# The scan's triangular inverse: block transposes on VectorE instead of TensorE, and b scaled to the chunk's end by GpSimd

## What is computed

```python
def step(state, inp):
    r_t, w_t, k_t, v_t, a_t, b_t = inp
    sa = jnp.einsum('bhij,bhj->bhi', state, a_t)
    state = (state * w_t[:, :, None, :] + sa[..., None] * b_t[:, :, None, :]
             + v_t[..., None] * k_t[:, :, None, :])
    return state, jnp.einsum('bhij,bhj->bhi', state, r_t)
```

## Time and profile before

| what | value |
|---|---|
| median of 3 runs | 1724.61 us (1722.05 to 1726.17) |
| span of the profiled execution | 1724.5 us, which is its own time from first to last instruction |
| TensorE busy | 1670.0 us, 97% |
| VectorE busy | 1327.7 us, 77% |
| ScalarE, GpSimd busy | 696.7 us, 614.6 us |
| mean granted TensorE clock | 0.991 |

### The profile page before, as it was taken

How to read it: one execution, slowest core, us unless ns; L and a number is a source line. 1 busy time by engine, 2 the same in 40 slices (tenths; PEclk the granted TensorE clock), 3 DMA queues, 4 the chain that set the end, 5 groups by cost and what they waited for, 6 DMA issues and landing times.

```text
span 1724.5 us, 29253 instructions
## 1 busy us (share of the span) xinstructions
PE 1670.0 (97%) x11467; PEld 1472.8 (85%) x11467; DVE 1327.7 (77%) x2704; ACT 696.7 (40%) x1056; POOL 614.6 (36%) x393
## 2 busy tenths in 40 slices
PE   9999899988999999999999999999999999999997
PEld 7877469977888898999989999999999998777886
DVE  5654665576599998999926667888888888887777
ACT  4112752233333344888833333333333333333334
POOL 0000011000376664332342235656556555442120
PEclk9999999999999999999999999999999999999999
DMA  6220010021323353566497788999999999999994
GB/s 241 97 93 17 1 51 4 4 111 57 115 101 115 121 161 130 194 231 247 175 369 277 237 306 332 354 372 350 339 353 371 354 340 323 356 387 334 328 314 175
DMA packets 128040, 380.89 MB, mean 221 GB/s; under 512 B 12064, under 2 KB 52384, under 8 KB 126880
## 3 DMA queue, kind: packets, MB, share of 16 engines
q1 hardware_dynamic: 81104, 207.28, 33.8%
q0 software_dynamic: 37728, 159.40, 25.0%
q10 hardware_dynamic: 9072, 12.35, 2.0%
HBM read 339.92 MB, written 39.06 MB: 220 GB/s over the span
## 4 chain that ended last, share of the span: by engine, by line
PE 45%; DVE 11%; DMA 4%; ACT 0%; issue 0%; POOL 0%; SPq 0%; DVEq 0%; ACTq 0%; POOLq 0%
PE ps L203 15%; PE ps L205 15%; PE ps L204 15%; DVE gated_cols L2130 5%; DMA mixed<-hidden_ahead 3%; DVE wout_raw L2130 3%; DVE wout_raw L2133 2%; PE ps L2248 1%; DMA gates<-gate_matrix 1%; DVE v_lo L2183 0%; DVE h L2205 0%; ACT v_hi L2094 0%; DVE h L2212 0%; POOL u_lo L1990 0%; DVE h L2153 0%
## 5 line engine op out<-in xcount | busy, mean ns | idle before, releaser
L203 PE MATMUL ps<-v_hi,a_hi 128*128 128x512 f32 x768 | 301.5, 393 | 10.7 <-DVE a_lo L2186 7.9
L204 PE MATMUL ps<-v_lo,a_hi 128*128 128x512 f32 x768 | 300.8, 392 | 0.0
L205 PE MATMUL ps<-v_hi,a_lo 128*128 128x512 f32 x768 | 300.6, 391 | 0.0
L2007 POOL DMA_INDIRECT v_selected<-in_v,expert_index x128 | 186.3, 1456 | 298.2 <-DVE h L2153 284.0
L203 PE MATMUL ps<-xn_hi,u_hi 128*128 128x384 f32 (+1 forms) x800 | 275.0, 344 | 9.3 <-DVE xn_lo L1425 3.7
L204 PE MATMUL ps<-xn_lo,u_hi 128*128 128x384 f32 (+1 forms) x800 | 272.1, 340 | 0.0
L205 PE MATMUL ps<-xn_hi,u_lo 128*128 128x384 f32 (+1 forms) x800 | 272.0, 340 | 0.0
L2183 DVE TENSOR_TENSOR v_lo<-wout_raw,v_hi 128x1024 fp32r<-128x1024 f32 x128 | 156.6, 1223 | 99.5 <-ACT v_hi L2094 98.4
L1998 POOL DMA_INDIRECT u_selected<-in_u_rows,expert_index x128 | 181.7, 1419 | 142.0 <-DVE hidden_selected L2140 114.7
L2094 ACT ACTIVATE v_hi<-wout_raw 128x1024 fp32r<-128x1024 f32 x128 | 135.0, 1054 | 137.4 <-PE ps L205 137.4
L203 PEld LDWEIGHTS ps<-v_hi,a_hi 128*128 128x128 f32 x768 | 145.1, 189 | 41.4 <-DVE v_lo L2183 12.8
(11 more groups left out here) (329 smaller groups left out, 3102.7 us busy)
## 6 DMA issues: line engine op xcount, KB each, us to landing
wq_raw<-in_u_t SPq DMA_DIRECT2D x128, 512.0 KB, 4.9
wout_raw<-in_v SPq DMA_DIRECT2D x128, 512.0 KB, 7.0
gate_matrix<-gate_stage POOLq DMA_DIRECT2D x6, 4096.0 KB, 14.1
gates<-gate_matrix SPq DMA_DIRECT2D x32, 768.0 KB, 8.4
win_raw<-in_win_t SPq DMA_DIRECT2D x25, 512.0 KB, 3.5
mixed<-hidden_ahead SPq DMA_DIRECT2D x60, 192.0 KB, 7.0
wq_raw<-in_wq_t SPq DMA_DIRECT2D x16, 512.0 KB, 3.5
hidden_ahead<-hidden_route ACTq DMA_DIRECT2D x30, 192.0 KB, 2.0
```

The lines of the kernel that those rows point to most:

```text
L203: nc.tensor.matmul(out, w_hi, m_hi, start=first, stop=False)
L204: nc.tensor.matmul(out, w_hi, m_lo, start=False, stop=False)
L205: return nc.tensor.matmul(out, w_lo, m_hi, start=False, stop=last)
L2007: pool.indirect_dma_start(v_sel[:, k % GB, :], None, v_rows, bass.IndirectOffsetOnAxis(S.expert[:, k:k + 1], 0)).then_inc(s_vsel[k % GB], 16)
```

## The change

On TensorE the transposes inside `inverses` go, with their semaphores, and ScalarE's copies of them. VectorE transposes instead, with its instruction for blocks of 32x32 elements, for two chunks in one instruction of 128 partitions x 512 elements: `tt` into `tc` ahead of level 0, and `tc` into `tt` behind each second add of the levels 0 to 3. Up to there the matrices are zero outside their diagonal blocks of 32x32. VectorE's other work in the levels moves behind the level's last transpose.

In the chain, the decay is applied to `pre` beforehand, and to b instead of to the product: GpSimd multiplies the chunk's columns of `S.bs` in place by `S.pc` (`to_chunk_end`, 128x256 elements) once `with_b` has read them, and `turn_b_and_k` waits for that (`s_bsp`). GpSimd's bonus multiplication moves from behind chunk 3's addition to the front of chunk 4, which is the same place in its order. The squares of the group norm go into `k_new`, so the second inverse waits for the bonus multiplication (`s_rk`).

```diff
@@ scan, GpSimd @@
+            def to_chunk_end(ch):
+                x = S.bs[:, :, ch * C:(ch + 1) * C]
+                pool.wait_ge(s_g1, ch + 1)
+                st.do(pool.tensor_tensor(x, x, bc(S.pc[:, :, ch], 2, C), ALU.mult), s_bsp)
+
             for ch in range(NCH):
+                half, c = divmod(ch, HC)
+                if c == 0 and half:
+                    pool.wait_ge(s_late, LATE_COUNT)
+                    st.do(pool.tensor_tensor(bonus, bonus, S.k_new[:, :, :], ALU.mult), s_rk)
+                to_chunk_end(ch)
                 pool.wait_ge(s_tt0, ch + 1)
                 st.do(pool.tensor_tensor(tt[:, ch], tt[:, ch], bc(eye, 1, HP), ALU.add), s_eye)
-                if ch == HC - 1:
-                    pool.wait_ge(s_late, LATE_COUNT)
-                    st.do(pool.tensor_tensor(bonus, bonus, S.k_new[:, :, :], ALU.mult), s_rk)
@@ scan, TensorE @@
             def turn_b_and_k(ch):
                 if earlier(ch):
                     pe.wait_ge(s_trev, 2 * earlier(ch))
+                pe.wait_ge(s_bsp, ch + 1)
...
                     for c in range(HC):
-                        ch = half * HC + c
                         if level == 0:
-                            pe.wait_ge(s_eye, ch + 1)
-                            by_head(cut(4 + c, 0, C), lambda j, h: tt[h, ch, j, :], unit).then_inc(s_turn, 1)
-                    for c in range(HC):
-                        if level == 0:
-                            pe.wait_ge(s_turned, n + c + 1)
+                            pe.wait_ge(s_turned, turned_count(half, 0, c))
                         else:
                             pe.wait_ge(s_yadd, n - HC + c + 1)
...
                     for c in range(HC):
+                        ch = half * HC + c
+                        pe.wait_ge(s_xc, n + c + 1)
                         if level:
-                            by_head(cut(4 + c, 0, HW), lambda j, h: tc[h, c, j, :],
-                                    lambda j, h: second(eye[h, :], m // 2)).then_inc(s_turn, 1)
-                    for c in range(HC):
-                        ch = half * HC + c
-                        pe.wait_ge(s_xbd, n + c + 1)
-                        pe.wait_ge(s_turned, n + c + 1)
+                            pe.wait_ge(s_turned, turned_count(half, level, c))
@@ scan, ScalarE @@
             def inverses(half):
                 for level in range(NL):
-                    for c in range(HC):
-                        ch = half * HC + c
-                        act.wait_ge(s_turn, HC * (half * NL + level) + c + 1)
-                        if level == 0:
-                            st.do(act.activation(tc[:, c], cut(4 + c, 0, C), ACT.Copy), s_turned)
-                            continue
...
@@ scan, VectorE @@
             def inverses(half):
+                def pair(e):
+                    return slice(half * HC + 2 * e, half * HC + 2 * e + 2), slice(2 * e, 2 * e + 2)
+
+                for e in range(HC // 2):
+                    chs, cs = pair(e)
+                    dve.wait_ge(s_eye, chs.stop)
+                    st.do(v.transpose(tc[:, cs].rearrange("p c j t -> p (c j t)"),
+                                      tt[:, chs].rearrange("p c j t -> p (c j t)")), s_turned)
...
-                        if half and c == 1 and level < NL - 1:
-                            norm_step(S, dve, v, st, level, 0)
-                        if not half and c == HC - 1 and level < 2:
-                            other_half((4, 2)[level])
+                        if level < NL - 1 and c % 2:
+                            chs, cs = pair(c // 2)
+                            st.settle()
+                            st.do(v.transpose(tt[:, chs].rearrange("p c j t -> p (c j t)"),
+                                              tc[:, cs].rearrange("p c j t -> p (c j t)")), s_turned)
+                    if half and level < NL - 1:
+                        norm_step(S, dve, v, st, level, 0)
+                    if not half and level < 2:
+                        other_half((4, 2)[level])
...
                 st.settle()
+                st.do(v.tensor_tensor(pre, pre, bc(S.pc[:, :, ch], 2, HD), ALU.mult))
+                st.settle()
                 beside(0)
                 dve.wait_ge(s_s, ch + 1)
                 st.do(v.tensor_tensor(new, pre, cut(0, FULL, C), ALU.add), s_snew)
-                st.settle()
-                st.do(v.tensor_tensor(new, new, bc(S.pc[:, :, ch], 2, HD), ALU.mult), s_snew)
                 st.settle()
                 beside(1)
...
             take_y(HC - 1)
+            dve.wait_ge(s_rk, 1)
             inverses(1)
```

More of the change, by code:

```diff
@@ L869, in scan @@
         tc, xz = sb("inverse", [P, HC, HP, C]), sb("level_products", [P, HC, HP, C])
-        S.y_sq = S.ks[:, 0:2, :].rearrange("p a (g i) -> p (a g) i", i=HD)
+        S.y_sq = S.k_new[:, 0:2, :].rearrange("p a (g i) -> p (a g) i", i=HD)
         st_s = S.zm[:, 13, :].rearrange("p (w j i) -> p w j i", w=2, j=HP)
@@ L879, in scan @@
                                                       sem("s_prev"), sem("s_eye"))
-        s_turn, s_turned, s_x, s_xbd, s_y, s_yadd = (sem("s_turn"), sem("s_turned"), sem("s_x"), sem("s_xbd"),
+        s_turned, s_x, s_xc, s_y, s_yadd = (sem("s_turned"), sem("s_x"), sem("s_xc"),
                                                      sem("s_y"), sem("s_yadd"))
+        s_bsp = sem("s_bsp")
         s_o1, s_o1c, s_u, s_uc, s_s, s_snew, s_yo, s_yc = (sem("s_o1"), sem("s_o1c"), sem("s_u"), sem("s_uc"),
@@ L899, in first, with turned_count @@
             return x.rearrange("p (b w m) -> p b w m", w=2, m=m)[:, :, 0, :]
-        def second(x, m):
-            return x.rearrange("p (b w m) -> p b w m", w=2, m=m)[:, :, 1, :]
+        def turned_count(half, level, c):
+            return (half * NL + level) * (HC // 2) + c // 2 + 1
         def banks(ch):
@@ L995, in inverses @@
                     pe.wait_ge(s_yc, HC)
-                    pe.wait_ge(s_snew, 2 * HC)
+                    pe.wait_ge(s_snew, HC)
                 for level in range(NL):
@@ L1030, in chain @@
                 if ch:
-                    pe.wait_ge(s_snew, 2 * ch)
+                    pe.wait_ge(s_snew, ch)
                 by_head(cut(0, 0, C), lambda j, h: S.ra[h, j, ch, 0, :], old).then_inc(s_o1, 1)
@@ L1162, in inverses @@
                         st.do(v.tensor_tensor(xz[:, c, :, 0:HW], cut(c, 0, HW), bc(S.const(f"level{level + 1}"), 1, HP),
-                                              ALU.mult), s_xbd)
+                                              ALU.mult), s_xc)
                     for c in range(HC):
```

## The result

| | before | changed |
|---|---|---|
| median, 20 runs each | 1721.98 us | 1730.44 us |
| lowest to highest | 1718.82 to 1729.88 | 1722.54 to 1739.88 |
| profiled execution, span | 1724.5 us | 1729.0 us |
| mean granted TensorE clock | 0.991 | 0.973 |
| scan, from the first `with_b` to the first matmul of `finish` | 126.2 us | 134.4 us |

The ratio is 1.0046, 95% interval 1.0034 to 1.0057: 8.5 us lost where the forecast was 12 to 15 gained. The scan alone is 8.2 us longer and so holds all of it. The shorter difference of the two profiled spans, 4.5 us, has 3.6 us of the later stages in it, less than the runs of one kernel differ by.

A forecast was written before the change was run, and what follows sets the result against it. TensorE, busy 97% of the span, was taken as the bound, except in the second half's chain. Terms -6.9 - 5.6 - 3.5 - 0.1 + 1.1 = -15.0 (unrounded -14.9) took 1724.5 to 1709.6 us; range for all 1705 to 1717.

The forecast's parts named there:

- Part 1: The two inverses: a plain level takes 3.73 us instead of 5.6, levels with other VectorE work 1.10 to 1.59 more.
- A lower clock: Granted clock below 1.00 in the inverses, listed only among what the profile would show if the forecast were wrong.
- First inverse -6.9, second -5.6: Inverses without TensorE's transposes: first 21.7 us instead of 28.6, second 24.3 instead of 29.9.
- The transpose, 0.69 us: VectorE's transpose of 128x512 f32 in the inverses, priced as an ordinary operation, bounds 0.43 and 1.22 us.
- half-rate transpose: Rival: VectorE's transpose of 4-byte elements takes 1.22 us, adding 8.2 us, time 1717.8; chance 0.12.
- a faster one: Rival: VectorE's transpose takes 0.43 us, so held-up levels each give 0.52 us more, time 1706.5; chance 0.03.
- one slower than 1.64 us: Rival: VectorE's transpose paces every level and the gain is gone; 1737.3 us at 2.44 us each; chance 0.03.
- The transpose blocks on GpSimd: Rival: level 2's first transpose is held 2.7 us by GpSimd's 4.52 us bonus multiplication, time 1712.1; chance 0.12.
- The chain -3.5 and -0.1: Decay moved ahead of the product: second half's chain 3.5 us shorter, first half's 0.1.
- GpSimd's scaling +1.1: Scaling b delays the first half's head: 0.9 us in chunk 0, 0.2 in chunk 1; bounds 0.9 and 2.9.
- The wait for `s_rk`, level 0's transposes, the square root: Second inverse's wait long met; level 0's transposes cost nothing, 1.4 us if uncovered; square root after step 3 as before.
- The sign and the chances: Whole kernel: faster 0.94, within 0.2% 0.03, slower 0.03; the forecast case itself 0.64.

The follow-up runs named there:

- e1_fill: Changed kernel plus unread 128x128 TensorE matmuls (fillers): 5 ahead of each inverse's first X, 4 between X and Y of levels with other VectorE work; 1707.19 us, ratio 0.9911.
- e2_chain_alone: Kernel before plus only the chain's part: decay on pre ahead of the product, b scaled by GpSimd, TensorE keeps its transposes; 1718.31 us, ratio 0.9979.
- e10_half_fill: Changed kernel with 2 unread 128x128 TensorE matmuls at each idle place, ahead of the inverses and in levels, instead of 5 and 4; 1708.93 us, ratio 0.9919.
- e6_fill_levels: Changed kernel with 4 unread 128x128 TensorE matmuls in each level with other VectorE work, none ahead of the inverses' first X; 1725.68 us, ratio 1.0017.
- e4_moved: Changed kernel, VectorE's other work moved behind the last level, 5 unread 128x128 matmuls ahead of each inverse, none in levels; 1712.15 us, ratio 0.9945.

## Why the prediction was wrong

**The failed step** is in Part 1: every burst of the levels was priced at 1.86 us, its duration at 2.4 GHz, and the clock was kept at 1.00 by a comparison at the end of the prediction, that the second chain held 1.00 with TensorE busy 17.68 of 21.75 us. That window consists of 64x64 and 128x256 matmuls; a level consists of 64x32 ones, and between these the gap of about 1 us that the change itself made dropped it each time the clock was still up (5 of 5). The row compared was of another kind of work. The windows of the inverses before were no support either: inside the levels TensorE had hardly any gap there, 28.19 of 28.60 us busy. A lower clock was named as a sign of error, but given no price and no chance, though its effect is larger than the whole gain.

What the runs showed in its place is 3.41 us instead of 1.86 for nine bursts of the second inverse and six of the first, with 3.1 us for a seventh. What it cost, by the changed kernel against e1_fill, which differs only in the fillers: first inverse 30.9 against 21.8 us (9.1), the chunk behind it 6.66 against 5.06 (1.6), second inverse 33.35 against 24.50 (8.9), the chunk behind it 6.74 against 4.20 (2.5), the head of the scan 20.27 against 19.52 (0.8): 22.9 us, and the scans differ by 134.4 - 111.8 = 22.6. The forecast's -14.9 and these +22.9 give +8.0; measured were 8.5 between the medians and 8.2 between the scans.

Point by point:
- *First inverse -6.9, second -5.6.* Right at 1.00: -6.8 and -5.4 in e1_fill.
- *The transpose, 0.69 us.* Measured 0.71 us, for 128x512 f32. The rivals of a half-rate transpose, of a faster one and of one slower than 1.64 us fall.
- *The transpose blocks on GpSimd.* It doesn't: in e1_fill one at 271.99 took 0.71 us beside the multiplication of 270.34 to 274.87. The Trainium skill (SBUF — State Buffer, "SBUF: two separate sides") has VectorE held only in a two-port mode or with two SBUF inputs; the trace agrees for this instruction of one input, if it runs in no such mode, which no run here shows.
- *The chain -3.5 and -0.1.* Right: 4.20 us a chunk instead of 5.27, the second half's chain 3.45 us shorter in e2_chain_alone (21.75 to 18.30), and its scan shorter by 2.3 us, where the sum with the head gave 2.5.
- *GpSimd's scaling +1.1.* Right: it takes 0.62 us rather than 0.73, and from the first `with_b` to the start of the inverse e1_fill has 19.5 us where the kernel before has 18.5. These rows of the changed kernel answer to the earlier trace rows; the 2.39 us of idle time at the stage's border and the slow `with_b` behind it are told below:

```profile
239.27 1.60 PEld L949 LDWEIGHTS ps<-r_and_a,b_scaled 64*64 64x64 f32 x16 [2.39 <-issue]
...
241.36 0.62 POOL L927 TENSOR_TENSOR b_scaled<-b_scaled,chunk_decay 128x256 f32<-128x256 f32 x1 [0.26 <-PE ps L949]
...
242.50 0.75 PEld L949 LDWEIGHTS ps<-consts_scan,b_scaled 64*64 64x64 f32 x16
```

- *The wait for `s_rk`, level 0's transposes, the square root.* At nothing, as said.
- *The sign and the chances.* Slower had 0.03, and for another reason. The clock should have been the rival on the other side: half clock from a gap on, with the bursts behind it nearly twice as long. What these rows couldn't tell was whether it would fall, but a case that could take more than the gain was not a case of 0.

What stays open: how long a gap, beside which work, the clock bears, and why the gap ahead of the first X passed four times and dropped it twice. e10_half_fill shows gaps of 0.27 to 0.70 us passing and the clock falling once soon after; no run here settles it. Nor did a run put wider matmuls around the same gaps, so that the narrowness of the levels' matmuls has a part in it is argued from the chain's window and not shown.

## What to carry to other kernels

When work is taken off TensorE, first ask what it does in the time that comes free: if it stands still there beside narrow matmuls, the price can be the clock of the whole stretch. In the trace, look at the granted clock by windows before looking at any wait, and at whether the same burst has kept its length. The remedy is cheap where the gap is waiting time anyway: fillers, or the other engine's work placed where it leaves no gap.

## What was not expected of the hardware

- Once at 1.2 GHz, bursts of 64x32 matmuls without any gap did not bring 2.4 GHz back: the changed kernel ran nine bursts at 3.41 us in its second inverse, TensorE busy 32.97 of 33.35 us, and only came back at about 358.5 us, among the chain's matmuls. In e6_fill_levels four fills of 128x128 matmuls, 2.07 us each, between such bursts did not bring it back either. The same bursts at 2.4 GHz without gaps held it for 16.8 us in e4_moved. The Trainium skill (TensorE: Matmul & The Clock Gate, "HAM oscillation") describes a kernel whose clock falls in the waits between its bursts. The runs agree in kind, with waits much shorter than that page's, and show besides that a TensorE that is busy by the profile may stay at the lower level.
- A burst of 64 of these matmuls takes 1.86 us at the upper level and 3.41 us at the lower, a factor of 1.83.
- The level at which a stage is entered differs from run to run by what came before: the changed kernel's scan began at the lower level, behind 2.2 us of idle time at the stage's border, and e1_fill's at the upper, with 0.3 us. At its head this made 0.8 us. In all ten traces a scan behind 2.2 us began low (four of them) and one behind 0.3 to 1.7 us began high (six).
